# Reordering the opening stages of a one-core transformer block: norm, adaLN columns, weight units and query rotations

## The reference

```python
mod = silu(c) @ w_ada + b_ada                       # 12288 columns; mod_c the same from c_ctx
sh1, sc1, g1, sh2, sc2, g2 = split(mod, 6)
h  = modulate(rms_norm(x,  norm_attn), sh1,  sc1)   # modulate(h, s, c) = h * (1 + c) + s
hc = modulate(rms_norm(ctx, norm_attn), sh1c, sc1c)
dq, dk, dv, sq, sk, sv = split(h @ w_in)            # 4608 columns; hc @ w_in for k and v
dq, dk, sq, sk = apply_rope(...)                    # latent tokens only
a  = concat(head_rms(diff_attention(...)), head_rms(window_attention(...))) @ w_out
x  = x + g1 * a
x  = x + g2 * peer(modulate(rms_norm(x, norm_ffn), sh2, sc2), ...)
return rms_norm(x, final_norm)
```

## Time and profile before

| | |
|---|---|
| median of 3 runs | 2205.82 us (2203.56 to 2205.92) |
| the profiled execution | 2209.09 us |
| its span, first to last instruction | 2207.3 us |
| TensorE busy | 2101.0 us, 95% of the span |
| VectorE busy | 1677.2 us, 76% |
| ScalarE busy | 1222.9 us, 55% |
| GpSimd busy | 297.2 us, 13% |
| mean granted TensorE clock | 0.973 of full speed |

### The profile page before, as it was taken

One profiled execution on the slowest core, in us unless ns is written; L12 is line 12 of the kernel. 1 busy time (PEld: TensorE's weight loads), 2 busy tenths in 40 slices (PEclk: granted clock), 3 DMA queues, 4 the chain that ended last, 5 costly groups with the idle time before them and its releaser, 6 DMA issues.

```text
span 2207.3 us, 42296 instructions
## 1 busy us (share of the span) xinstructions
PE 2101.0 (95%) x13442; PEld 1857.9 (84%) x13442; DVE 1677.2 (76%) x2954; ACT 1222.9 (55%) x2243; POOL 297.2 (13%) x264
## 2 busy tenths in 40 slices
PE   3899999898999999999999999999879999999996
PEld 0478888666989999999999999999668888888885
DVE  5377767787666488878787687887568988888886
ACT  2232234486445567676776565556446666666662
POOL 0000000000000000000001211111344443222220
PEclk7899999899999999999999999999989999999997
DMA  9878876400675455555598644444769999999982
GB/s 386 333 280 284 282 259 241 157 1 1 239 256 165 150 183 179 184 185 178 184 343 304 206 156 158 157 160 156 263 231 355 367 343 350 346 348 361 374 330 74
DMA packets 160892, 524.74 MB, mean 238 GB/s; under 512 B 34960, under 2 KB 35776, under 8 KB 160192
## 3 DMA queue, kind: packets, MB, share of 16 engines
q1 hardware_dynamic: 123840, 452.63, 57.1%
q0 software_dynamic: 20576, 67.20, 9.0%
q10 hardware_dynamic: 16416, 4.19, 0.9%
HBM read 515.52 MB, written 8.39 MB: 237 GB/s over the span
## 4 chain that ended last, share of the span: by engine, by line
PE 88%; DVE 5%; DMA 4%; issue 1%; POOL 1%; ACT 1%; SPq 0%; DVEq 0%; ACTq 0%
PE PS L780 70%; PE PS L1093 10%; PE PS L1037 2%; DMA ada_t<-w_ada 2%; DMA values_scratch<-A 1%; PE PS L936 1%; DVE st L1331 1%; DMA raw<-stream 1%; PE PS L910 1%; PE PS L823 1%; PE PS L787 1%; PE PS L763 1%; POOL picked L413 1%; PE PS L924 1%; DVE w_lo L1130 0%
## 5 line engine op out<-in xcount | busy, mean ns | idle before, releaser
L437 ACT ACTIVATE w_hi<-raw 128x512 fp32r<-128x512 f32 x1088 | 682.8, 630 | 714.6 <-PE PS L780 553.5
L1130 DVE TENSOR_TENSOR w_lo<-raw,w_hi 128x512 fp32r<-128x512 f32 x1088 | 733.8, 690 | 342.4 <-ACT w_hi L437 322.7
L780 PE MATMUL PS<-h_h,w_hi 128*128 128x256 f32 (+1 forms) x2304 | 658.7, 286 | 3.1 <-DVE h_l L1160 2.1
L780 PE MATMUL PS<-h_l,w_hi 128*128 128x256 f32 (+1 forms) x2304 | 653.6, 284 | 0.0
L780 PE MATMUL PS<-h_h,w_lo 128*128 128x256 f32 (+1 forms) x2304 | 653.6, 284 | 0.0
L780 PEld LDWEIGHTS PS<-h_h,w_hi 128*128 128x128 f32 x2304 | 444.0, 193 | 4.2 <-issue 2.6
L780 PEld LDWEIGHTS PS<-h_l,w_hi 128*128 128x128 f32 x2304 | 444.1, 193 | 0.0
L780 PEld LDWEIGHTS PS<-h_h,w_lo 128*128 128x128 f32 x2304 | 443.7, 193 | 0.0
L780 PE MATMUL PS<-w_hi,p_hl 128*128 128x512 f32 x1024 | 400.5, 391 | 21.5 <-DVE w_lo L1130 21.1
L780 PEld LDWEIGHTS PS<-w_hi,p_hl 128*128 128x128 f32 x1024 | 192.9, 188 | 65.6 <-issue 23.2
L780 PE MATMUL PS<-w_lo,p_hl 128*128 128x512 f32 x512 | 199.7, 390 | 0.0
(11 more groups left out here) (228 smaller groups left out, 2847.2 us busy)
## 6 DMA issues: line engine op xcount, KB each, us to landing
raw<-stream SPq DMA_DIRECT2D x544, 512.0 KB
raw_far<-stream SPq DMA_DIRECT2D x104, 512.0 KB
ada<-w_ada SPq DMA_DIRECT2D x96, 512.0 KB, 4.4
ada_t<-w_ada SPq DMA_DIRECT2D x64, 512.0 KB, 9.4
ada_u<-w_ada SPq DMA_DIRECT2D x32, 512.0 KB, 5.7
values_scratch<-A ACTq DMA_DIRECT2D x1, 2560.0 KB, 18.9
x_c<-x_ctx SPq DMA_DIRECT2D x1, 2048.0 KB, 7.7
x<-x_lat SPq DMA_DIRECT2D x1, 2048.0 KB, 15.1
```

What stands on the lines that cost most here:

```text
L437: nc.scalar.activation(w_hi[:, (2 * j + hf) % SPLIT, :], ring[:, j, hf * HALF:(hf + 1) * HALF], ACT.Copy).then_inc(S["w_high"], 1)
L780: ins = mm(out_, l_, r_, start=(start and q == 0), stop=(stop and q == 2), skip_group_check=check)
L1130: V_.tensor_tensor(w_lo[:, h % SPLIT, :], ring[:, h // 2 % RAW, at_:at_ + HALF], w_hi[:, h % SPLIT, :].bitcast(F32), ALU.subtract).then_in ...
```

## The change

1. The small loads are cut in two. The three that the first turn and modulation need (bias, norms, identity; 144 KB) get a semaphore of their own, `mod_in`, and are issued behind `ada1(1)`. The other seven are issued behind `ada1(5)`, and VectorE waits for them only ahead of the lambda products.
2. Units 0 and 1 are issued ahead of `ada1(4)`, units 2 and 3 ahead of `ada1(7)`, units 4 and 5 ahead of `ada1(11)`; units 6 and 7 stay behind `ada1(15)`.
3. On TensorE, `sum_partitions(1)` and `ada_turn(0)` stand right behind pair 7, and pairs 8 to 11 behind them.
4. VectorE rotates the two blocks of a query chunk apart: the first behind the fourth half of the next chunk, the second two halves later.
5. After chunk 8 TensorE does `ada_columns(4)` first, then turns chunk 7's queries, scores pair 0, and turns chunk 8's queries after that.

```diff
+        MOD_LOADS = [(b_ada[:], parv["b_ada"]), (norms[:], par[:, PAR["norm_attn"][0]:PAR["head_gain"][1]]),
+                     (ident[:], conv["ident"])]
+        SMALL_LOADS = [(silu_c[:], ...),
                        (nsink[:, 0, :], parv["sink"]), (lam_v[:], ...),
...
             ada1(1)
+            for dst, src in MOD_LOADS:
+                sp.dma_start(dst, src).then_inc(S["mod_in"], 16)
             ada1(2)
-            for dst, src in SMALL_LOADS[1:]:
-                sp.dma_start(dst, src).then_inc(S["par_in"], 16)
             ada1(3)
-            for g in range(1, GROUPS):
-                ada1(4 * g)
-                ada1(4 * g + 1)
-                unit((g - 1) // 2, 2 * (g - 1) % 4, first=g < 3)
-                unit((g - 1) // 2, 2 * (g - 1) % 4 + 1, first=g < 3)
-                ada1(4 * g + 2)
-                ada1(4 * g + 3)
+            for a in range(4, 16):
+                if a in (4, 7, 11):
+                    u = 2 * (4, 7, 11).index(a)
+                    unit(u // 4, u % 4, first=u < 4)
+                    unit(u // 4, u % 4 + 1, first=u < 4)
+                if a == 6:
+                    for dst, src in SMALL_LOADS[1:]:
+                        sp.dma_start(dst, src).then_inc(S["par_in"], 16)
+                ada1(a)
             unit(1, 2)
             unit(1, 3)
...
                 if g == 0:
-                    pe.wait_ge(S["par_in"], N_SMALL)
+                    pe.wait_ge(S["mod_in"], 48)
                     pe.wait_ge(S["norm_sqrt"], 2)
...
             ada_products(8, 16)
+            sum_partitions(1)
 
             for g in range(1, GROUPS):
                 n = KT * g
+                if g == 1:
+                    ada_turn(0)
                 ada_products(n, n + 4)
-                if g == 1:
-                    sum_partitions(1)
-                ada_turn(g - 1)
+                if g > 1:
+                    ada_turn(g - 1)
                 ada_products(n + 4, n + 8)
...
-                if c >= 6:
+                if 6 <= c < 8:
                     turn_queries(c - 6)
-            turn_queries(3)
+            pe.wait_ge(S["evac_d"], EVAC_DC[8])
             ada_columns(4, 4, acc)
+            turn_queries(2)
...
+            pe.wait_ge(S["turn_q_kept"], 6)
+            score_pair(0)
+            turn_queries(3)
             pe.wait_ge(S["turn_q_kept"], 8)
-
-            score_pair(0)
...
-                if kind == "q":
+
+            def evac_query(c, q):
+                if q == 0:
+                    dve.wait_ge(S["w_free"], 16 * (c + 1) + SPLIT)
                     if c - 5 >= 2:
                         dve.wait_ge(S["turn_q"], 2 * (c - 5 - 1))
-                    for q in range(QT):
-                        rope(Qt[:, (c - 5) % 2, q, :], PS[:, banks[q], :], q, 512)
+                rope(Qt[:, (c - 5) % 2, q, :], PS[:, BANKS[c][q], :], q, 512)
...
-                        if b == 2 * c and j == 1:
+                        if c >= 6 and b == 2 * c and j in (1, 2):
+                            evac_query(c - 1, j - 1)
+                        elif b == 2 * c and j == 1:
                             evac(c - 1)
...
-            evac(8)
+            evac_query(8, 0)
+            evac_query(8, 1)
```

More of the change, by code:

```diff
@@ L86, in block_program @@
     with ExitStack() as ctx:
-        sem_names = ("cc_in par_in x_in xc_in keys_in x2_in x2_out out_done "
+        sem_names = ("cc_in mod_in par_in x_in xc_in keys_in x2_in x2_out out_done "
                      "silu ada1_used ada1_col ada2_used ada_row_kept ada_col ada_col_kept ada_zeroed ada_sum "
@@ L230, in block_program @@
         conv = {n: con[:, a:b] for n, (a, b) in CON.items()}
-        SMALL_LOADS = [(silu_c[:], parv["cc"].rearrange("p (k c) -> p k c", c=2)), (b_ada[:], parv["b_ada"]),
-                       (norms[:], par[:, PAR["norm_attn"][0]:PAR["head_gain"][1]]),
+        MOD_LOADS = [(b_ada[:], parv["b_ada"]), (norms[:], par[:, PAR["norm_attn"][0]:PAR["head_gain"][1]]),
+                     (ident[:], conv["ident"])]
+        SMALL_LOADS = [(silu_c[:], parv["cc"].rearrange("p (k c) -> p k c", c=2)),
                        (nsink[:, 0, :], parv["sink"]), (lam_v[:], parv["lam_qk"].rearrange("p (a d) -> p a d", a=4)),
-                       (ident[:], conv["ident"]), (iota[:], conv["iota"]), (iota16[:], conv["iota16"]),
+                       (iota[:], conv["iota"]), (iota16[:], conv["iota16"]),
                        (cs[:, 0], conv["cos"].rearrange("p (q d) -> p q d", q=QT)),
@@ L1190, in modulation @@
                 if g == 0:
-                    dve.wait_ge(S["par_in"], N_SMALL)
+                    dve.wait_ge(S["mod_in"], 48)
                 cols = PS[:, ADA1_TURN[g % 2], :].rearrange("p (k q h r) -> p q h k r", k=GT, q=2, h=2)
@@ L1241, in _ @@
                 modulate_and_split(k)
+            dve.wait_ge(S["par_in"], N_SMALL)
             link(V_.tensor_tensor(lam_v[:, 0, :], lam_v[:, 0, :], lam_v[:, 1, :], ALU.mult))
```

## The result

The changed kernel took 2189.45 us (median of 4 runs, 2186.85 to 2190.8) against 2205.87 for the kernel before in the same set of runs: a ratio of 0.9926, interval [0.9913, 0.9939]. One of the four executions of the kernel before, at 8812.14 us, is left out of the ratio; without it the median before is 2205.82. The forecast was 2187.0, range 2182 to 2193. The profiled execution took 2190.8 us with a span of 2189.0, that is 18.3 us less than before in both; the forecast sum was 18.8.

A forecast was written before the change was run, and what follows sets the result against it. The chain is 88% TensorE work, so gains lie only where it leaves TensorE: opening 9.9 + rotations 2.7 + scores 6.2 = 18.8 us, and 2205.8 - 18.8 = 2187.0 us, range 2182 to 2193.

The forecast's parts named there:

- the three places: Where the chain leaves TensorE: opening up to 124.93 us, rotations of two query chunks, chunk 8's end to first score maxima.
- Opening, 9.9 forecast: Opening stage: half 12 starts at 115.0 us in place of 124.93, a gain of 9.9 us, bounds 7.4 and 11.9.
- half 12 starts between 97.1 + 16.5 = 113.6 and 97.1 + 18.7 = 115.8: Opening: half 8 starts at 97.1 us; to half 12 takes 18.70 us at present, 2.21 of it half 8's lower clock.
- each tile's slot is free some 4 us or more before its transfer's turn: Opening, loads ahead of half 8: the ring of eight is no obstacle; pair 27's slots are the tightest.
- rival A: Every TensorE restart begins at the lower clock: gain 8.8 + 2.7 + 5.2 = 16.7 us, total 2189.1 us; chance 0.22.
- Rotations, 2.7 forecast: Chunks 7 and 8: splitting the rotations cuts each TensorE stop of about 1.6 us; gain 2.7 us, bounds 2.2 and 3.2.
- Scores, 6.2 forecast: After chunk 8: third maxima at 425.8 or 427.8 us in place of 433.02; gain 7.2 or 5.2, middle 6.2 us.
- if the shift were smaller at the end than at 433 us: Sign of being wrong: the third maxima were to come some 18 us earlier than 433.02, the program's end shifting alike.
- the forecast case: Whole kernel: opening 9.9, rotations 2.7 and scores 6.2 us sum to 18.8 us, giving 2187.0 us; chance 0.55.
- B: Loads fall below 410 GB/s without the ring's pause: at 385 the opening gains 4.5 to 5 us, total 2192.3; chance 0.12.
- C: Modulation is held by something other than the sum, so the opening's gain is gone: 8.9 us, total 2196.9; chance 0.07.
- D: Slower: TensorE stays at 1.2 GHz through chunk 0, each half 2.5 us longer, total 2219 for all sixteen; chance 0.02.

The follow-up runs named there:

- the two other traces of the old opening: Kernel before with only the rotations' edit (half 12 at 126.98 us, median 2205.20 us) and with only the scores' edit (126.82 us, median 2202.04 us).
- the second trace: The changed kernel run once more with no further edit; half 12 at 115.58 us, median 2189.31 us, ratio 0.9922 to the kernel before.
- the two other traces of the old order: Kernel before with only the opening's edits (2194.89 us) and with only the rotations' edit (2205.20 us); scores' stretch 17.81 us in both.
- the finer orders: Changed kernel with units 1, 3, 5 issued later singly (2188.17 us), with seven small loads last (2188.04 us), with both (2186.64 us, again 2187.80 us).

## Why the prediction was right

The time lies in the stated range, and the runs bear out the three places and what happens at each. How near the sum came is in part luck, as the sizes below show.

**How sure the sizes are.** The pieces' medians, each against the kernel before, are 11.5 us for the opening, 1.2 for the rotations and 4.3 for the scores, 17.0 together; the whole change is 16.4. By the ratios they are 9.9 (6.4 to 13.7), 0.9 and 4.4, together 15.2, against 16.3. So the pieces add up, but the forecast of 18.8 is 2.4 us more than the medians show. The 18.3 of the profiled executions sets an execution 3.3 us above the median of its runs against one 1.35 above.

**Opening, 9.9 forecast, 9.2 measured** against the kernel before's trace; against the two other traces of the old opening it is 11.1 to 11.3. The moved sum brought what it was said to (sum 37.0, half 0 at 49.8), and putting it back costs 4.9 us at half 12. Half 12 at 115.72 lies in "half 12 starts between 97.1 + 16.5 = 113.6 and 97.1 + 18.7 = 115.8", but the reason given for that step was incomplete, and half 8 was 1.0 late:

- The prediction took half 8 to half 12 as TensorE's own work and a choice of clock. Pair 31's landing stands in it as well. By the count of tiles it is 3.9 + 78 x 1.28 + 2.0 = 105.7, which the prediction didn't work out; in the second trace it was 107.5. There half 8 ran at full clock from 97.5, which by the prediction would give half 12 at 114.0. It came at 115.58, and 1.36 us of the difference is the wait for pair 31.
- Pair 27 landed at 96.5 and not 95.5. "each tile's slot is free some 4 us or more before its transfer's turn" was not so: in the changed kernel's chain pair 27's tiles are issued at 90.5, when pair 23 is done, and take 5.62 us to land. From 92 to 98 us the DMA moved 377, 322 and 377 GB/s, which is 0.75 us of transfers less than at 410. The rest of the 1.8 us by which pair 31 is late, about 1 us, I have not placed.

Two numbers of the sums have no working that gives them. The upper bound of 11.9 for the opening would be 124.93 - 113.6 = 11.3 by the step above, and rival A's opening of 8.8 would be 124.93 - 115.8 = 9.1. Neither changes the forecast.

**Units.** In the changed kernel they were hidden, as forecast, and the experiment shows that their place is worth 3.4 us at half 12, given the rest of the change. The small loads' cut is worth 0.1, which is nothing.

**Rotations, 2.7 forecast, 2.95 measured** in the changed kernel, 3.1 alone. The first rotation, two halves, then the second leave no marked stop.

**Scores, 6.2 forecast, 6.9 in this trace**, but 5.2 in most against the kernel before's trace, and 4.2 against the two other traces of the old order. So the middle and the lower bound of 5.2 were too high: the old order's third maxima don't always wait for scores at the lower clock, as the trace before had it. Which size it is hangs on the clock; in the changed kernel it stayed at 1.00 at 408 us. 9.21 + 2.95 + 6.94 = 19.10, the measured shift of the third maxima.

**After that.** The shift was taken as constant, and "if the shift were smaller at the end than at 433 us" was named as a sign of being wrong. It was smaller: 19.1 at the third maxima, 19.4 at 451.96 us (471.32 before), 17.7 at the output projection (532.74 against 550.47) and 18.3 at the end. The 1.6 us are lost at one place:

```profile
486.00:488.00 2.00, 0.75 (x6) 0.43 (x4) 1.78 (x8) 1.38 (x5) 0.00 (x0) 1.00 0.00 0
488.00:490.00 2.00, 2.00 (x19) 2.00 (x18) 1.87 (x4) 0.15 (x2) 0.00 (x0) 0.89 0.00 0
490.00:492.00 2.00, 2.00 (x8) 1.29 (x8) 0.85 (x2) 1.38 (x3) 0.00 (x0) 0.50 0.00 0
```

The kernel before has the same pause there (TensorE busy 0.74 us of 505.36 to 507.36) and kept 1.00 behind it. So it is the clock, at a place that the change doesn't touch, and not a wait that the change brought.

**The rivals.** A (restarts at the lower clock) gave 2189.1 and is the nearest to 2189.45; its reason held for the scores in most traces and for half 8 in one of two, where it then cost nothing that shows at half 12. The measured time can't tell A from the forecast case. The rule of the Trainium skill's TensorE: Matmul & The Clock Gate (HAM oscillation — how this bites in real kernels) fits the 4.26 and 4.03 us of halves 0 and 8 here; half 4, at 2.97, and halves 0 and 8 at full clock in the second trace don't follow it. B fell: 393 to 418 GB/s were held from 50 to 92 us. C fell, since the opening kept its 9.2 us, and D too: half 1 is back at 2.94 us (TensorE's chain of the changed kernel, half 1 at 55.13).

## What to carry to other kernels

Where a ring of loads and a matmul order are written by hand, count the bytes that must land ahead of every point at which the engine can wait, the last one too: making an earlier point sooner moves the wait to the next. Move the instruction that starts a chain (here one small sum) ahead of work that is only paced by loads; that alone was worth 4.9 us at half 12, more than the units' 3.4. Judge pieces of a few microseconds by stretches between two marks of the trace as well as by run times, which spread over 7 to 10 us here, and first find out how well each stretch repeats, in the kernel before too. The rotations' stretch repeated to 0.13 us in all ten traces that had the new order. Half 12 of the old opening spread over 2 us and the scores' stretch over 1 to 2 us, so one trace of each kernel doesn't size those pieces. A small sum moved sooner at half 8 or 12 need not show in the time: the finer orders brought half 12 forward by up to 2.3 us in a trace, and no version is shown to be faster for it.

## What the runs showed of the hardware that was not expected

TensorE's clock falls or stays for the same instructions with the same pauses. A place that the change doesn't touch, ahead of the query projection, in the kernel before and in the kernel with the rotations alone, set against each other by the start of that projection (660.39 and 657.97):

```profile
658.00:660.00 2.00, 0.26 (x2) 0.00 (x0) 1.96 (x5) 1.01 (x3) 0.00 (x0) 1.00 0.89 272
660.00:662.00 2.00, 1.61 (x7) 1.61 (x8) 0.94 (x3) 0.30 (x1) 0.00 (x0) 0.61 0.92 367
662.00:664.00 2.00, 2.00 (x12) 2.00 (x11) 0.00 (x0) 0.60 (x1) 0.00 (x0) 0.54 0.02 4
```

```profile
655.58:657.58 2.00, 0.25 (x2) 0.00 (x0) 1.97 (x5) 1.02 (x3) 0.00 (x0) 1.00 0.77 229
657.58:659.58 2.00, 1.61 (x13) 1.62 (x14) 0.93 (x3) 0.29 (x1) 0.00 (x0) 1.00 0.95 377
659.58:661.58 2.00, 2.00 (x19) 2.00 (x18) 0.69 (x1) 1.08 (x2) 0.00 (x0) 1.00 0.02 4
```

Busy times agree to 0.01 us up to the start, then 0.61 and 0.54 stand against 1.00. From that start to the next long stretch (764.30 and 760.37) the one takes 103.9 us and the other 102.4. Such differences of 1 to 2 us at several places can make a part of the spread between executions; how much of it they make was not tested, and what decides between the two clocks is not shown.
